# Second block's entry in a two-block kernel: order of the last scatter, of its sums and of the pairs' scatters

## The reference, cut to what matters

```
gate, idx = top_k(affinity, cap)            # 16 experts, 64 tokens each
hid = silu(xe @ w_gate[e]) * (xe @ w_up[e])
ye  = (hid @ w_down[e]) * gate
x   = x + g2 * scatter_add(ye, idx)         # by expert
x   = rms_norm(x, final_norm_g)             # end of the first block
h   = rms_norm(x, g_mix_norm_2)             # start of the second
z   = h @ w_in_2                            # keys, values, queries, gates, convolution
```

## Time and profile before

| what | value |
|---|---|
| time, median of 3 runs | 1929.61 us (1927.2 to 1934.13) |
| the profiled execution: its own time | 1930.07 us |
| the profiled execution: its span | 1928.8 us |
| PE busy in the span | 1734.6 us, 90% |
| DVE busy | 792.2 us, 41% |
| ACT busy | 571.5 us, 30% |
| stretch of the eight expert pairs | from about 740 us to 1201 us in the span |
| last scatter, norm sums, first chunks | about 1201 us to 1257 us |

### The profile page before, as it was taken

The page is one execution under the profiler, slowest core; times in us unless marked ns, Lnnn a source line. Parts: engine busy times, 40 slices in busy tenths (PEclk is TensorE's granted clock), DMA queues, the critical chain, the costliest instruction groups (busy, mean ns, idle before and its releaser), DMA issues.

```text
span 1928.8 us, 20338 instructions
## 1 busy us (share of the span) xinstructions
PE 1734.6 (90%) x8150; PEld 1128.5 (59%) x8150; DVE 792.2 (41%) x1325; ACT 571.5 (30%) x1026; POOL 118.0 (6%) x123
## 2 busy tenths in 40 slices
PE   5999899886999996999988888799888899999999
PEld 2656567564877772333333333587545678888877
DVE  2164754457633532210211202428477544444443
ACT  2224553555343331110110100331454542222221
POOL 0002121012100001000000000000100001011010
PEclk9999899888999998999999999899999999999999
DMA  8221201123323267999999999153400122222301
GB/s 308 95 67 44 88 22 44 66 88 131 106 69 132 102 269 285 425 423 423 423 424 425 424 423 413 59 171 87 131 1 1 44 87 88 88 87 94 115 10 44
DMA packets 93185, 329.40 MB, mean 171 GB/s; under 512 B 7828, under 2 KB 22820, under 8 KB 68516
## 3 DMA queue, kind: packets, MB, share of 16 engines
q1 hardware_dynamic: 86032, 315.80, 42.2%
q10 hardware_dynamic: 5716, 8.05, 1.3%
q0 software_dynamic: 1344, 4.25, 0.6%
HBM read 322.83 MB, written 4.20 MB: 170 GB/s over the span
## 4 chain that ended last, share of the span: by engine, by line
PE 70%; DVE 10%; DMA 9%; ACT 7%; issue 3%; ACTq 0%; SPq 0%; POOL 0%; DVEq 0%
PE PS L671 21%; PE PS L814 11%; PE PS L1060 9%; PE PS L412 7%; DMA room<-in_w_exp_gate_dram 7%; PE PS L408 3%; PE PS L543 3%; PE PS L825 3%; PE PS L625 3%; PE PS L887 2%; PE PS L468 1%; DMA room<-in_w_exp_down_dram 1%; PE PS L697 1%; PE PS L511 1%; DVE wR L1790 1%
## 5 line engine op out<-in xcount | busy, mean ns | idle before, releaser
L1790 DVE TENSOR_TENSOR wR<-ring,wR 128x1024 fp32r<-128x1024 f32 (+2 forms) x134 | 151.2, 1130 | 231.9 <-ACT wR L1175 231.8
L1175 ACT CAST wR<-ring 128x1024 fp32r<-128x1024 f32 (+2 forms) x134 | 129.9, 971 | 212.5 <-PE PS L1060 128.3
L1060 PE MATMUL PS<-wR,hR 128*128 128x512 f32 x768 | 177.9, 393 | 9.0 <-DVE tmp L2565 7.0
L671 PE MATMUL PS<-xR,wR 128*128 128x512 f32 x768 | 175.6, 389 | 0.9 <-DVE wR L1790 0.9
L1060 PEld LDWEIGHTS PS<-wR,hR 128*128 128x128 f32 x768 | 144.7, 189 | 42.2 <-DVE tmp L2565 9.8
L671 PEld LDWEIGHTS PS<-xR,wR 128*128 128x128 f32 x768 | 144.0, 188 | 31.1 <-issue 1.3
L671 PE MATMUL PS<-hR,wR 128*128 128x512 f32 x528 | 128.2, 404 | 10.6 <-DVE wR L1790 5.6
L814 PE MATMUL PS<-ring,xeT 128*64 128x512 f32 x512 | 115.5, 601 | 10.6 <-DMA ring<-in_w_exp_gate_dram 7.8
L814 PE MATMUL PS<-room,xeT 128*64 128x512 f32 x512 | 114.0, 593 | 11.9 <-DMA room<-in_w_exp_gate_dram 11.9
L671 PEld LDWEIGHTS PS<-hR,wR 128*128 128x128 f32 x528 | 102.4, 195 | 36.9 <-issue 9.3
L671 PE MATMUL PS<-hR1h,wR 128*128 128x512 f32 x320 | 102.2, 394 | 2.4 <-DVE wR L1790 2.4
(11 more groups left out here) (469 smaller groups left out, 2677.8 us busy)
## 6 DMA issues: line engine op xcount, KB each, us to landing
ring<-in_w_exp_gate_dram SPq DMA_DIRECT2D x32, 1024.0 KB, 26.5
room<-in_w_exp_gate_dram SPq DMA_DIRECT2D x32, 1024.0 KB, 25.9
ring<-in_w_exp_up_dram SPq DMA_DIRECT2D x32, 1024.0 KB, 26.3
room<-in_w_exp_up_dram SPq DMA_DIRECT2D x32, 1024.0 KB, 25.9
ring<-in_w_exp_down_dram SPq DMA_DIRECT2D x32, 1024.0 KB, 26.4
room<-in_w_exp_down_dram SPq DMA_DIRECT2D x32, 1024.0 KB, 27.6
ring<-in_w_mod_dram SPq DMA_DIRECT2D x12, 2048.0 KB, 8.0
ring<-in_w_in_dram SPq DMA_DIRECT2D x11, 2048.0 KB, 9.2
```

What stands on the lines that cost most here:

```text
L671: mm = T.matmul(b, o[s][:, k, :], x(t, k), start=(k == ks[0] and j == 0), stop=(k == ks[-1] and j == 2))
L1060: mm = T.matmul(down[m], uR[:, r % 2, s, k, 128 * i:128 * i + 128], o[t][:, 0, 512 * q:512 * q + 512], start=(k + j == 0), stop=(k == 3 an ...
L1175: A.copy(parts(wR, chunks, n)[0], W.view(unit)[:, ks, cs]).then_inc(act_hi.sem, act_hi.up(key))
L1790: V.tensor_tensor(lo, W.view(unit)[:, ks, cs], hi.bitcast(F32), ALU.subtract) \
```

## The change

PE: the scatter of pair p-1 moves from before the up product of pair p to behind it (and behind the turning of the next pair's tokens). In the last scatter, half 0 of the sums moves from behind tile 5 to behind tile 7. DVE: the additions of pair p-1 move behind the product that makes `hid` of pair p. In the last scatter the addition of tile k+1 stands ahead of the low term of tile k, and the low weight part of chunk 0 comes behind low term 4 and ahead of addition 6. ACT: the cast of each tile stands ahead of its square. The squares have six buffers, so squares 6 and 7 alone wait for half 0 of the sums. The 8 scalings of `xT` stand singly at the end of steps n = 5 to 12 of the second block instead of all behind raw 1.

```diff
@@ -291,7 +291,8 @@
     xR3, tmp = m11.take("xR3", [128, 2, 8, 512], F32R), m11.take("tmp", [128, 4, 512])
     uR = hR3[:, :, :, :].rearrange("p x (s k) t -> p s x k t", s=2)
     xo = mixT[:, :, :].rearrange("p (i q) n -> p i q n", q=2)
-    squares2 = [sq[:, 0, :], sq[:, 1, :]] + [xeT[:, 4 * i:4 * i + 4].rearrange("p k e s -> p (k e s)")[:, 0:512] for i in range(2)]
+    squares2 = [sq[:, 0, :], sq[:, 1, :]] + [xeT[:, 4 * i:4 * i + 4].rearrange("p k e s -> p (k e s)")[:, 512 * j:512 * j + 512]
+                                                   for i in range(2) for j in range(2)]
     squares3 = [sq[:, 0, :], sq[:, 1, :], tmp[:, 0, :], tmp[:, 1, :]]
     cN, rm, cT, eps = sq[:, 0, :], sq[:, 1, :], ss[:, 0:4], ss[:, 7:8]
     bmod = colA[:, 64:112]
@@ -679,7 +680,7 @@
             for total, mat in zip(totals, mats):
                 for k in range(4 * n, 4 * n + 4):
                     r = 32 * (k % 4)
-                    mm = T.matmul(total[r:r + 32, :], mat(k), tiles[k % 4], start=(n == 0), stop=(n == 1))
+                    mm = T.matmul(total[r:r + 32, :], mat(k), tiles[k % len(tiles)], start=(n == 0), stop=(n == 1))
             mm.then_inc(sem.sem, sem.up(key))
 
         def gate_tiles(pool):
@@ -824,17 +825,17 @@
                     T.wait_ge(*dve_moe["ye", p, 1])
                     T.matmul(b, ye[:, p % 2, 128 * k:128 * k + 128], PT[:, p % 2, :], start=True, stop=True) \
                         .then_inc(pe_moe.sem, pe_moe.up(("sc", p, k)))
-                    if total and k == 5:
-                        total2(0)
+                if total:
+                    total2(0)
 
             expert_in(0)
             for p in range(8):
                 pair_product("gate", p, xeT[:, :, p % 2, :], dve_moe["silu", p])
-                if p:
-                    scatter(p - 1)
                 pair_product("up", p, xeT[:, :, p % 2, :], dve_moe["hid", p])
                 if p < 7:
                     expert_in(p + 1)
+                if p:
+                    scatter(p - 1)
                 for hf in range(2):
                     b = every.take(T, ("hT", p, hf), act_moe["hT", p, hf])
                     T.wait_ge(*dve_moe["hid", p])
@@ -1515,11 +1516,11 @@
             A.wait_ge(*pool_moe["gmat"])
             for k in range(8):
                 A.wait_ge(*dve_moe["x", 7, k])
-                if k >= 4:
-                    A.wait_ge(*pe_moe["sums", 0])
-                A.activation(squares2[k % 4], xT[:, k, :], ACT.Square).then_inc(s.sem, s.up(("sq", k)))
                 A.activation(hR2[:, 0, k], xT[:, k, :], ACT.Copy, scale=AB[:, 1, k:k + 1]) \
                     .then_inc(s.sem, s.up(("h3", k)))
+                if k >= 6:
+                    A.wait_ge(*pe_moe["sums", 0])
+                A.activation(squares2[k % 6], xT[:, k, :], ACT.Square).then_inc(s.sem, s.up(("sq", k)))
                 if k == 3:
                     A.wait_ge(*pe_moe["down", 7, 3])
                     copy_hi(wR2, sec_chunks, 0)
@@ -2280,30 +2281,34 @@
             s = dve_moe
 
             def scatter(p):
-                for k in range(8):
-                    V.wait_ge(*pe_moe["sc", p, k])
-                    if p:
-                        V.wait_ge(*dve_moe["x", p - 1, k])
-                    V.scalar_tensor_tensor(xT[:, k, :], bank(("sc", p, k))[:, 0:512], modc[:, 40 + k, 0:1], xT[:, k, :],
-                                           ALU.mult, ALU.add).then_inc(s.sem, s.up(("x", p, k)))
-                    if p == 7:
-                        V.wait_ge(*act_moe["h3", k])
-                        V.scalar_tensor_tensor(hR2[:, 1, k], xT[:, k, :], AB[:, 1, k:k + 1], hR2[:, 0, k].bitcast(F32),
-                                               ALU.mult, ALU.subtract).then_inc(s.sem, s.up(("h3", k)))
-                        if k == 4:
-                            sub_lo(wR2, sec_chunks, 0)
+                for k in range(9):
+                    if k < 8:
+                        V.wait_ge(*pe_moe["sc", p, k])
+                        if p:
+                            V.wait_ge(*dve_moe["x", p - 1, k])
+                        V.scalar_tensor_tensor(xT[:, k, :], bank(("sc", p, k))[:, 0:512], modc[:, 40 + k, 0:1], xT[:, k, :],
+                                               ALU.mult, ALU.add).then_inc(s.sem, s.up(("x", p, k)))
+                    if k and p == 7:
+                        low(k - 1)
+                    if k == 5 and p == 7:
+                        sub_lo(wR2, sec_chunks, 0)
+
+            def low(k):
+                V.wait_ge(*act_moe["h3", k])
+                V.scalar_tensor_tensor(hR2[:, 1, k], xT[:, k, :], AB[:, 1, k:k + 1], hR2[:, 0, k].bitcast(F32),
+                                       ALU.mult, ALU.subtract).then_inc(s.sem, s.up(("h3", k)))
 
             V.wait_ge(s_iot, 16)
             for p in range(8):
                 V.wait_ge(*act_moe["sig", p])
                 V.tensor_tensor(hid, hid, bank(("moe", "gate", p)).rearrange("t (p k) -> t k p", k=8), ALU.mult) \
                     .then_inc(s.sem, s.up(("silu", p)))
-                if p:
-                    scatter(p - 1)
                 V.wait_ge(*pe_moe["up", p, 3])
                 V.wait_ge(*dve_moe["silu", p])
                 V.tensor_tensor(hid, hid, bank(("moe", "up", p)).rearrange("t (p k) -> t k p", k=8), ALU.mult) \
                     .then_inc(s.sem, s.up(("hid", p)))
+                if p:
+                    scatter(p - 1)
                 if p >= 2:
                     V.wait_ge(*pe_moe["sc", p - 2, 7])
                 V.tensor_scalar(PT[:, p % 2, :].rearrange("p (a b) -> p a b", a=2), iot, giT[:, 1, p:p + 1], None,
@@ -2330,10 +2335,6 @@
                         V.wait_ge(*pe_sec["cN"])
                         V.tensor_copy(cT, bank("cN")[:, 0:512].rearrange("p (i t) -> p i t", i=4)[:, :, 0]) \
                             .then_inc(s.sem, s.up("cT"))
-                        for k in range(8):
-                            V.wait_ge(*dve_moe["h3", k])
-                            V.scalar_tensor_tensor(xT[:, k, :], xT[:, k, :], colA[:, 32 + k:33 + k], rinv, ALU.mult,
-                                                   ALU.mult).then_inc(s.sem, s.up())
                 elif key[0] == "conv":
                     c = key[1]
                     if c in (0, 1):
@@ -2389,6 +2390,11 @@
                     after(sec_chunks[0][0])
                 if n > 1:
                     after(sec_chunks[n - 1][0])
+                if 5 <= n < 13:
+                    k = n - 5
+                    V.wait_ge(*dve_moe["h3", k])
+                    V.scalar_tensor_tensor(xT[:, k, :], xT[:, k, :], colA[:, 32 + k:33 + k], rinv, ALU.mult, ALU.mult) \
+                        .then_inc(s.sem, s.up())
 
         def select():
             s = dve_sel
```

## The result

| | before | changed |
|---|---|---|
| median | 1930.39 us (6 runs, 1926.9 to 1934.1) | 1912.51 us (6 runs, 1908.6 to 1918.9) |
| ratio of the times | | 0.9917, 95% interval 0.9901 to 0.9933 |
| profiled execution | 1930.07 us, span 1928.8 | 1913.68 us, span 1912.4 |

The change is faster by 16.0 us (0.8%), between 12.9 and 19.1 by the interval; 14.2 was forecast. The chip ran the changed kernel once more in the experiments: 1912.60 us, ratio 0.9908 (0.9888 to 0.9928).

A forecast was written before the change was run, and what follows sets the result against it. Experts were taken as bound by weight transfers, with engine waits behind the last landing. +3.0 - 12.5 - 4.7 = -14.2 us on 1930.07 gave 1915.9, said as 1916 us; range 1911 to 1922.

The forecast's parts named there:

- rival of starved transfers: Pairs 1 to 6: down slots freed late empty the transfer queue, 26.4 us more, 1942 us; chance 0.03.
- Part 1: Pairs' scatters behind the up products: free in pairs 1 to 6, last down product ends 3.0 us later.
- Part 2: Last scatter reordered: from its first product to the end of the sums 15.9 us instead of 28.4, gain 12.5 us.
- DVE is never idle: Last scatter: from low term 0 on DVE works without pause, 1.35 us a tile.
- the pace of DVE: Last scatter: 16 DVE operations and the weight part separate raw 0 from the scatter, late next after the change.
- The clock term: Raw 0's first half: full clock behind a 2.1 us gap, 3.0 us instead of 5.32, 2.3 us of the gain.
- The rival that the forecast gave a chance of 0.14: Raw 0: the 2.1 us gap brings half clock, 2.3 to 4.2 us of gain lost, 1918.2 to 1920.1 us; chance 0.14.
- Part 3: Scalings moved to steps 5 to 12: PE's 3.45 us wait before kv's second chunk goes, gain 4.7 us in all.
- The half clock in kv's second chunk: Second block: without the wait ahead of it, this chunk takes 3.2 us instead of 4.5, 1.3 us less.
- The cover of the scalings: Steps 5 to 12: scalings fit in DVE's idle time and cost nothing; uncovered, 0.67 us each, 5.4 us in all.
- its own range: Whole kernel: 1913.5 to 1918.5 us if the forecast's main case holds, set by the spread of single runs.
- The sign of a last landing later than 1195.6 us: End of pair 7: last expert weights landing after 1195.6 us would show the forecast wrong.

The follow-up runs named there:

- pair 7 alone in the old order: Changed kernel, but the scatter of pair 6 again ahead of pair 7's up product on PE and DVE: 1919.56 us, ratio 0.9945.
- without part 1: Changed kernel with the scatters of pairs 0 to 6 put back ahead of the up products: ratio 0.9921.
- square-first version: Changed kernel, but ACT squares each tile ahead of its cast, as before: ratio 0.9949.
- additions not ahead: Changed kernel, but DVE makes each low term right behind its own addition, weight part behind low term 4: ratio 0.9967.
- wider gap: Changed kernel, but the low weight part of chunk 0 stands behind low term 6, so raw 0 waits for it: one run, 1913.3 us.
- part 1 alone: Kernel before, with only the scatters of pairs 0 to 6 moved behind the up products: 1934.11 us, ratio 1.0018.

## Why the prediction was right, point by point

**What bounds it.** Right. The DMA share stayed at 1.01 to 1.02 through all pairs, and neither the late slots of pairs 1 to 6 nor PE's shorter waits moved the last landing. The rival of starved transfers is refuted by the share and by the version with pair 7 alone in the old order.

**Part 1, +3.0 us.** Down ended 6.4 to 6.6 us behind the last landing instead of 3.8: +2.6 to +2.8. The path of the changed kernel is only 1.0 us longer than without part 1, because raw 0's first products ran at full clock in the one and not in the other; the forecast has no such term, and that the order of pair 7 brings it is not shown.

**Part 2, -12.5 us.** Measured -12.6 in the changed kernel: raw 0 at 10.95 (11.05 worked out), first half 3.01 (3.0), end of the sums 15.8 (15.9). The additions ahead are its largest share (5.4 us). The forecast worked out the new times from the first tile on, so it did not need to know what made up the old 28.4 us, and it names neither the half clock of half 0 nor ACT's wait for it (1.7 us). Its words "DVE is never idle" and "the pace of DVE" are too simple: its own times have low term 4 waiting for cast 4, and the chain goes over ACT up to there. The clock term, 2.3 us, came true in all three executions with pair 7 in the new order, but in part by luck. The reason given, that 2.1 us is nearer to 1.59 than to 4.06, was too weak: the same gap cost 1.2 to 1.6 us in four other versions. The rival that the forecast gave a chance of 0.14 is what these four show, at a smaller size than its 2.3 to 4.2 us.

**Part 3, -4.7 us.** Measured -5.2. The half clock in kv's second chunk was right (1.3 us by the starts of the chunks in both traces). Too small were two others. The second chunk starts 2.95 us behind the first without the wait and 6.56 us with it, so the wait was worth 3.6 us and not the 3.45 us of idle time; and the lower clock reached 0.25 us into the third chunk. As the kv wait above shows, the clock's share was that of one execution: before it could have been 0.1 or 2.4 us as well. The cover of the scalings held.

**The sum.** -14.2 forecast, -15.2 on the three distances, -16.0 in time. The median, 1912.5, lies 3.5 us under the forecast of 1916, and 1.0 us outside its own range of 1913.5 to 1918.5. Of the 3.5 us, 1.0 us is in the terms; the rest is within the interval of the ratio and less than the scatter of stretches that the change doesn't touch. That scatter was put at 2.5 us either way for the forecast's own range, which was too small: single runs of the changed kernel went from 1906.7 to 1918.9.

**The signs named in advance** came as told: down's last quarter does not wait for DMA, additions and low terms alternate at 0.66 us, raw 0 starts at 10.95 us behind a gap of 1.99 us, there is no wait ahead of kv's second chunk, and the DMA share stays full. Down ends 2.6 to 2.8 us later where 3.0 was named. One of the signs of being wrong, a first half of raw 0 of over 5 us, came in none of the executions with the 2.0 us gap, but in the square-first version (5.5 us). The sign of a last landing later than 1195.6 us was given in absolute time and can't be used so: in the second profile it came at 1197.9 us, with the stretch before the experts 2.3 us longer than before.

## What to carry to other kernels

In a ring of operations across two engines, count what each engine does per turn; putting the next turn's first operation ahead of this turn's last takes the crossing of signals out, and the pace becomes the busier engine's own (here from 2.73 to 1.32 us a tile). Move work that nobody waits for out of the place where the list is being waited for, to places behind which the next signal is late anyway. Where transfers set the pace, an order that fills every wait only shifts the backlog, and the backlog is paid once, behind the last transfer: the last round may want another order than the others.

## What the runs showed of the hardware that was not expected

A gap of 2.0 us ahead of the same 12 products left the granted clock at 1.00 in three executions (3.0 us) and brought it to 0.62 to 0.68 over the half in four others (4.2 to 4.6 us), with the same order of engines right ahead of it in all seven. Nor does the length of a longer gap order the loss: 2.9 us (additions not ahead) and 4.0 us (wider gap) gave 4.6 us, 3.0 us (square first), 3.7 us (part 1 alone) and 4.1 us (before) gave 5.3 to 5.5. One wait of 3.45 us, ahead of kv's second chunk, was followed by full clock in one execution and by 1.2 GHz in another.

The Trainium skill, "TensorE: Matmul & The Clock Gate", says in its part on the clock gate that the same kernel can differ from run to run in when the clock changes. The wait ahead of kv's second chunk agrees with that (a loss of 0.1 to 2.4 us). At raw 0 the split goes with the order of pair 7, three executions against four, and whether that is more than chance stays open. So in this kernel the clock's share at one place is known from a single profile only to within 1 to 2 us.
